# One transfer, one rounding copy and one subtraction per weight step, in place of two halves each

## The reference

```python
n = rms_norm(x, attn_norm_g)
proj = n @ w_in                                   # stages conv and rest
...
h = x + jnp.concatenate([gla_out, nsa_out], axis=-1) @ w_out      # stage out
m = rms_norm(h, ffn_norm_g)
return h + (jax.nn.silu(m @ w_gate) * (m @ w_up)) @ w_down        # stages up0 to down2
```

## Time and profile before

| | us |
|---|---|
| three runs | 2448.64, 2455.42, 2455.43 |
| median | 2455.42 |
| profiled execution, first to last instruction (its span) | 2443.0 |
| mean granted TensorE clock | 0.920 |

### The profile page before, as it was taken

One profiled execution on the slowest core, in us unless ns is written; L12 is line 12 of the kernel. 1 busy time (PEld: TensorE's weight loads), 2 busy tenths in 40 slices (PEclk: granted clock), 3 DMA queues, 4 the chain that ended last, 5 costly groups with the idle time before them and its releaser, 6 DMA issues.

```text
span 2443.0 us, 45011 instructions
## 1 busy us (share of the span) xinstructions
PE 2199.2 (90%) x16718; PEld 2127.6 (87%) x16718; DVE 1576.2 (65%) x2077; ACT 995.4 (41%) x1230; POOL 0.2 (0%) x4
## 2 busy tenths in 40 slices
PE   5999987489799999999999996999689998888997
PEld 5999986369799999999999985999378998888997
DVE  5888564548787577764767576346656766666544
ACT  4346631333355632343333344223245633424642
POOL 0000000000000000000000000000000000000000
PEclk8999966569899999999999997999699998998998
DMA  4767521007567586765878682357003875444552
GB/s 174 245 239 270 184 80 44 0 1 241 172 220 236 174 287 227 263 226 186 269 259 273 200 294 85 100 181 273 6 1 127 271 248 171 138 138 142 185 181 95
DMA packets 119530, 433.76 MB, mean 178 GB/s; under 512 B 13216, under 2 KB 13600, under 8 KB 119216
## 3 DMA queue, kind: packets, MB, share of 16 engines
q1 hardware_dynamic: 119472, 432.98, 53.2%
HBM read 430.83 MB, written 2.10 MB: 177 GB/s over the span
## 4 chain that ended last, share of the span: by engine, by line
PE 69%; DVE 16%; DMA 8%; issue 4%; ACT 2%; SPq 1%; DVEq 1%; ACTq 0%
PE ps L411 19%; PE ps L413 19%; PE ps L412 19%; DMA side<-w_side 8%; DVE w_lo L1002 3%; PE ps L643 2%; PE ps L473 2%; PE ps L468 1%; DVE sq L1064 1%; PE ps L480 1%; DVE mod_sum L1014 1%; DVE at_max L1339 1%; PE ps L512 1%; PE ps L437 1%; PE ps L632 1%
## 5 line engine op out<-in xcount | busy, mean ns | idle before, releaser
L411 PE MATMUL ps<-a_hi,w_hi 128*128 128x256 f32 x3280 | 939.8, 287 | 58.4 <-DVE w_lo L1002 33.4
L412 PE MATMUL ps<-a_lo,w_hi 128*128 128x256 f32 x3280 | 934.2, 285 | 0.0
L413 PE MATMUL ps<-a_hi,w_lo 128*128 128x256 f32 x3280 | 933.8, 285 | 0.0
L776 ACT ACTIVATE w_hi<-raw 128x1024 fp32r<-128x1024 f32 x610 | 634.2, 1056 | 699.3 <-PE ps L413 636.0
L1002 DVE TENSOR_TENSOR w_lo<-raw,w_hi 128x1024 fp32r<-128x1024 f32 x610 | 718.8, 1220 | 108.3 <-ACT w_hi L776 105.6
L411 PEld LDWEIGHTS ps<-a_hi,w_hi 128*128 128x128 f32 x3280 | 635.8, 194 | 66.1 <-DVE w_lo L1002 35.5
L412 PEld LDWEIGHTS ps<-a_lo,w_hi 128*128 128x128 f32 x3280 | 636.0, 194 | 0.0
L413 PEld LDWEIGHTS ps<-a_hi,w_lo 128*128 128x128 f32 x3280 | 635.8, 194 | 0.0
L411 PE MATMUL ps<-b_hi,w_hi 128*128 128x256 f32 x1664 | 485.0, 291 | 17.6 <-DVE w_lo L1002 8.4
L413 PE MATMUL ps<-b_hi,w_lo 128*128 128x256 f32 x1664 | 473.8, 285 | 0.0
L412 PE MATMUL ps<-b_lo,w_hi 128*128 128x256 f32 x1664 | 473.7, 285 | 0.0
(11 more groups left out here) (242 smaller groups left out, 1462.6 us busy)
## 6 DMA issues: line engine op xcount, KB each, us to landing
raw<-w_main SPq DMA_DIRECT2D x610, 512.0 KB, 4.3
side<-w_side SPq DMA_DIRECT2D x200, 512.0 KB, 5.6
x_tok<-x_in SPq DMA_DIRECT2D x4, 512.0 KB, 6.0
ctx_tok<-ctx_tok SPq DMA_DIRECT2D x1, 2048.0 KB, 9.2
y_out<-o_tok SPq DMA_DIRECT2D x4, 512.0 KB, 2.7
cons<-cons_in SPq DMA_DIRECT2D x1, 542.0 KB, 8.0
table<-counts_tab SPq DMA_DIRECT2D x1, 512.0 KB, 10.1
table<-masks_in SPq DMA_DIRECT2D x1, 448.0 KB, 11.1
```

The costliest lines, as they stand in the source:

```text
L411: pe.matmul(out_ap, wh, act_hi[:, kt, :], start=first and n == 0, stop=False)
L412: pe.matmul(out_ap, wh, act_lo[:, kt, :], start=False, stop=False)
L413: mm = pe.matmul(out_ap, wl, act_hi[:, kt, :], start=False, stop=last and n == len(blocks) - 1)
L776: act.activation(w_hi[:, slot, :], raw[:, slot, :], ACT.Copy).then_inc(hi_ready, 1)
```

## The change

The unit of the weight stream becomes the step. One DMA brings both halves (1 MB, `128x2x1024`), one ScalarE copy rounds 128x2048, one VectorE subtraction makes `w_lo` of 128x2048, and TensorE waits once per step. `hi_ready` and `lo_ready` count steps; `halves_used` still counts halves, and `hi` now waits until both halves of the step two before are used. Slots, buffers, the matmuls, the side stream and the order of the steps on each engine stay as they are.

```diff
-            for h in range(4):
-                sp.dma_start(raw[:, h, :], w_main[h]).then_inc(raw_full[h], 16)
+            for h in range(0, 4, 2):
+                sp.dma_start(raw[:, h:h + 2, :], w_main[h:h + 2].rearrange("a p n -> p a n")).then_inc(raw_full[h // 2], 16)
...
-            def load(i, h):
+            def load(i, s):
-                sp.wait_ge(lo_ready, i * 4 + (h - 3))
-                src = w_main[h] if isinstance(i, int) else w_main[bass.ds(i * 4 + h, 1)].rearrange("a p n -> (a p) n")
-                sp.dma_start(raw[:, h % 4, :], src).then_inc(raw_full[h % 4], 16)
+                sp.wait_ge(lo_ready, i * 2 + (s - 1))
+                src = w_main[2 * s:2 * s + 2] if isinstance(i, int) else w_main[bass.ds(i * 4 + 2 * s, 2)]
+                slot = 2 * (s % 2)
+                sp.dma_start(raw[:, slot:slot + 2, :], src.rearrange("a p n -> p a n")).then_inc(raw_full[s % 2], 16)
...
-                        for half in range(2):
-                            load(i, 2 * (s0 + k + c) + 4 + half)
+                        load(i, s0 + k + c + 2)
...
+                pe.wait_ge(lo_ready, i * 2 + (s + 1))
                 for c in range(2):
-                    pe.wait_ge(lo_ready, i * 4 + (2 * s + c + 1))
...
             def hi(i, s):
-                for c in range(2):
-                    slot = 2 * (s % 2) + c
-                    act.wait_ge(raw_full[slot], i * 16 + 16 * (s // 2 + 1))
-                    if s >= 2:
-                        act.wait_ge(halves_used, i * 4 + (2 * s + c - 3))
-                    act.activation(w_hi[:, slot, :], raw[:, slot, :], ACT.Copy).then_inc(hi_ready, 1)
+                slots = slice(2 * (s % 2), 2 * (s % 2) + 2)
+                act.wait_ge(raw_full[s % 2], i * 16 + 16 * (s // 2 + 1))
+                if s >= 2:
+                    act.wait_ge(halves_used, i * 4 + (2 * s - 2))
+                act.activation(w_hi[:, slots, :], raw[:, slots, :], ACT.Copy).then_inc(hi_ready, 1)
...
             def lo(i, s):
-                for c in range(2):
-                    slot = 2 * (s % 2) + c
-                    dve.wait_ge(hi_ready, i * 4 + (2 * s + c + 1))
-                    dve.tensor_tensor(w_lo[:, slot, :], raw[:, slot, :], w_hi[:, slot, :].bitcast(F32), ALU.subtract)\
-                       .then_inc(lo_ready, 1)
+                slots = slice(2 * (s % 2), 2 * (s % 2) + 2)
+                dve.wait_ge(hi_ready, i * 2 + (s + 1))
+                dve.tensor_tensor(w_lo[:, slots, :], raw[:, slots, :], w_hi[:, slots, :].bitcast(F32), ALU.subtract)\
+                   .then_inc(lo_ready, 1)
```

More of the change, by code:

```diff
@@ L285, in build @@
         ident, ones = con("ident"), con("ones")
-        raw_full = [S(f"raw_full{j}") for j in range(4)]
+        raw_full = [S(f"raw_full{j}") for j in range(2)]
         side_full = [S(f"side_full{j}") for j in range(2)]
@@ L730, in _ @@
                 for c in range(2):
-                    pe.wait_ge(lo_ready, 2 * s + c + 1)
+                    pe.wait_ge(lo_ready, s + 1)
                     for n in range(2):
```

## The result

The changed kernel takes 2476.18 us (median of 4 runs, 2472.59 to 2481.63), the kernel before in runs beside it 2454.01 us (4 runs, 2448.64 to 2455.43). The ratio is 1.0108, with a 95% interval of 1.0076 to 1.0141: slower, by 22 us between the medians and by 26 by the ratio (19 to 35). That is only about 1% of the time, but clear of the noise. The forecast was 2505. The direction and the range held; the size was twice too large.

The account below looks back on a forecast made before the run. TensorE, busy 90%, was taken as bounding, with the side-transfer loop (11.78 us against 11.5) in some stages. Loops 30, table loads 10 and starts 10 made +50 on 2455.4, so 2505 us; range 2463 to 2540.

Parts of the forecast that it names:

- Loops through side: Weight load waits for the whole subtraction, so side lands later and loops through it lengthen: 30 us, ends -19 and +61.
- the choice of +0.6 between -0.57 and +1.07: Growth per side loop: -0.57 if data move at 370 GB/s, +1.07 if landing keeps 7.67 us from first issue; +0.6 taken.
- Side landing "7.2 to 7.4 us after the end": Sign in the changed profile: side lands 7.2 to 7.4 us after the subtraction ends, against 6.70 before.
- the wait "well over 153": Sign in the changed profile: VectorE's wait for the side transfer rises well over 153 us.
- the share "above 8%": Sign: the side transfer's share of the chain that ended last rises above 8%, from 7.6%.
- wrong if side lands in under 6.5: Stated refutation: the prediction is wrong if side lands under 6.5 us, or TensorE's waits for `w_lo` don't grow.
- three leads of 1.4: In up1, up2 and out, 24 loops lose 4.8 us in all, less TensorE's three leads; some 2 us left.
- Table loads: Silu table load ahead of the merged copy stalls TensorE: 4 us in up0's second half, 6 in od_z, together 10.
- Dry starts: Where TensorE has run dry it waits for both halves: 7.5 us at seven starts, 2.6 for three late copies, together 10.
- At nothing: SP's saved issue, half the semaphore traffic, 0.1 us per copy, and TensorE's single wait outside the starts: no effect.
- the fourth rival: Worse than the upper end: all hundred or so loops bound, the weights ring too; 2545 us or more, chance 0.08.
- the first rival: The 1 MB transfer pays back: loops grow by 0, fixed losses of 20 us, perhaps 5 less, remain; 2465 to 2478, chance 0.18.

Follow-up runs that it names:

- e4: Kernel before, still two 512 KB loads per step, but the first half's load also waits until both halves are subtracted: 2470.49 us, ratio 1.0072.
- e1: Kernel before with one 1 MB load per step behind the whole subtraction; copies, subtractions and TensorE's waits stay halves: 2451.29 us, ratio 0.9996.
- e3: Changed kernel with subtraction and TensorE's wait in halves again; 1 MB load and merged copy stay: 2462.88 us, ratio 1.0037.
- e5: Kernel before with one edit, TensorE waiting once per step for both subtracted halves: 2467.12 us, ratio 1.0075.
- e6: Changed kernel with six dummy matmuls keeping TensorE busy before the starts of ev_kv and od_u: 2475.85 us, ratio 1.0108.
- e10: Kernel before with only the issue order turned, side half ahead of the two half weight loads of the same step: 2414.54 us, ratio 0.9848.
- e9: Changed kernel with the side half's load issued ahead of the same step's 1 MB load: 2451.15 us, ratio 1.0006.
- e2: Changed kernel with the megabyte as two 512 KB loads, both behind the whole subtraction: 2489.60 us, ratio 1.0157.

## Why the prediction was right in direction and wrong in size

- **Loops through side: forecast 30 (ends -19 and +61), measured about 0.** This is the step that failed, the choice of +0.6 between -0.57 and +1.07. The upper end rested on the idea that three halves need the same 7.67 us from their first issue. They don't: side lands 6.0 us after its own issue in before (201.96 to 207.97) and in after (200.83 to 206.83), whether the weights ahead went out 1.66 us earlier or 0.58. e4 has the delay without the larger transfer and shifts side by 0.25 in place of 1.07; e1 has both, and the run is equal to before. Why the 1.1 us by which the first load went out sooner bought so little stays open. By stage it is the same: the steps of the stages with a side stream, the second half of up0 left out, grew by no more than about 1 us in all. Side landing "7.2 to 7.4 us after the end" was 6.75, the wait "well over 153" was 132, the share "above 8%" was 6.2%. The bound "wrong if side lands in under 6.5" wasn't crossed, but the landing is nearer to it than to the value taken. The 30 also hold a slip: 4.8 less three leads of 1.4 is 0.6, where some 2 were taken.
- **Table loads: forecast 10, measured about 7.** In od_z two steps take 11.98 us. ACT in after, against the earlier trace rows:

```profile
2284.19 1.28 ACT L763 ACT_TABLE_LOAD   x1 [2.46 <-PE ps L413]
...
2296.17 1.28 ACT L763 ACT_TABLE_LOAD   x1 [2.32 <-PE ps L413]
```

  Before, two steps took 11.5; eight times 0.48 is 3.8, and the stage grew by 3.6 (forecast 6). In the second half of up0 two steps grew by 0.45, 3.6 in all (forecast 4), though the whole stage only by 1.7. With halves of the subtraction (e3) the stall in od_z is gone. ev_z, where the prediction held the stall to be covered, grew by 2.5, with three waits of TensorE for `w_lo` of 0.35 us, where before had none: a part of it got through.
- **Dry starts: forecast 10, measured more.** ev_kv and od_u alone grew by 10.8. PE at od_u's start in after, against the earlier trace rows:

```profile
2112.99 0.55 PE L411 MATMUL ps<-a_hi,w_hi 128*128 128x256 f32 x1 [2.95 <-DVE w_lo L1000]
```

  The gap grew from 1.03 to 2.95, by the 1.07 + 0.87 of the working almost exactly (1.92). What the working lacked is the clock behind the gap, 1.5 us where it falls (e5, e6). It doesn't fall at each gap: within od_u after gained 1.5 us of clock at a later gap against before. In ev_kv 1.4 of the 5.1 us lie ahead of the start, at a gap of 1.60 us in both kernels. The six us behind it, in before and then in after:

```profile
1522.80:1528.80 6.00, 4.79 (x25) 3.37 (x26) 6.00 (x16) 3.74 (x9) 0.00 (x0) 1.00 0.00 0
1531.70:1537.70 6.00, 5.67 (x25) 4.60 (x26) 6.00 (x16) 3.74 (x9) 0.00 (x0) 0.72 0.00 0
```

  e6, up to there the same code as after, has 1.00 like before, so this part can't be put down to the change. e5, with the gaps of the single wait alone, costs 18 us instead of 7.5. In all, TensorE's waits for `w_lo` came to 58 us where some 90 were forecast.
- **At nothing: the merged copy.** The copies' own 0.1 us and SP's issues were worth nothing, as said. But the subtraction now waits for the whole copy, and that was counted only at three starts, behind the table loads and in the fourth rival, with "weights landing 5.6 us after issue ... makes 10, under 11.5". That holds for steps of 5.75 us; in down2 two steps take 9.5 where nothing holds them up (e10). e3 against e1 puts 10 to 12 us on the merged copy. In the profiles of the two, rest (4.1), down0 and down2 (2.6 each), ev_kv (2.2) and od_u (2.1) grew most.
- **The sum.** 0 + 7 + about 18 + the copy would be more than 22, so the pieces overlap. That a loop which waits for side has room for a later subtraction would explain it, and e9 agrees: without these loops the same pieces cost 37 us. No run tests the overlap by itself. In part the total was saved by luck, as errors of opposite sign met: the loops were put 30 us too high, the starts and the copy too low.
- On the term that failed: the Trainium skill, "DMA: Bandwidth & Descriptors", asks for transfers of 1 MiB or more (section Bandwidth) and has each transfer pay a fixed part (section Anatomy of one DMA, which measured its fit on transfers issued by GpSimd; these are issued by SP). e1 against e4 and after against e2 agree with the rule, with 19 and 13 us for one transfer in place of two. The fit gives 5.6 us for the three halves, an estimate by that page; from the first issue to the addition the trace has 6.58, about 1 us more.
- The chances: the first rival, 2465 to 2478 with the loop at 0 and the fixed losses at 15 to 20, is what came, and had 0.18. For the upper end I had one row, in which the first load's early issue may have been of no use; that row couldn't tell whether the time ran from the first issue or from side's own. The other reading was there: the earlier trace rows give 6.0 from side's issue just as well as 7.67 from the first one. Of two readings of one row I took the dearer for most of the sum.

## What to carry over

When a transfer is late in a loop, count its time from its own issue as well as from the first one ahead of it, and look at what stands ahead of it in its queue: here the order of two issues was worth 37 us (1.5%), with no change to any size. Merging halves saves instructions on engines that wait anyway, and takes from the engine that does not wait the half-step at which it could begin. A gap of 1 us on TensorE that grows to 2 or 3 can cost 1.5 us more than the difference, as the clock behind it may fall; but it falls behind some gaps and not behind others of the same length, so take its price from the granted clock behind each gap and not from the gap alone.

## What the runs showed of the hardware

- Granted clock behind a gap of TensorE: 1.00 in the six us after gaps of 0.83 and 1.03 us, 0.72 after gaps of 1.97, 2.17, 2.75 and 2.95 us; 1.00 again where matmuls of no use filled the gap. But a gap of 3.05 us had 1.00 behind it in after and 0.74 in e6, and in e9 ten us at 1.2 GHz began behind a gap of 0.96 us and small matmuls.
- One load of 1 MB lands 4.8 us after its issue (median of 305), one of 512 KB in 4.3 (610). The same bytes in half as many transfers took 114647 packets in place of 119530; 305 x 16 = 4880 of those missing are under 512 B (8336 against 13216).
- In rest, the addition that waits for a transfer of 512 KB begins 5.6 to 6.0 us after the transfer's own issue (before, e1, e4, after), with 1 MB queued ahead of it as one load or two, over 0.58 to 1.66 us. The shortest of these landings over the whole span take 3.0 to 3.2 us.
- The granted clock in the sparse attention, where TensorE starts and stops, varies between executions of one kernel (0.61 and 0.75 in the same 48 us), for 16 us of that stretch. Two profiled executions can't be subtracted as a whole; stage by stage they can, to within some 2 us here.
